# A new order for the input LayerNorm's first blocks, and two out projection tiles in two parts each

## What is computed

```python
x = layer_norm(x, ln_in_g, ln_in_b)                 # the input LayerNorm
proj = x @ w_in                                     # 1024 -> 2304 columns, four token mixers read them
...
out = jnp.concatenate([ya, yb, yc, yd], axis=-1) @ w_out     # yc is the attention's quarter
x = layer_norm(ALPHA * x + mix, ln1_g[l], ln1_b[l])
x = layer_norm(ALPHA * x + sq_relu_mlp(x, w_ff1[l], w_ff2[l]), ln2_g[l], ln2_b[l])
```

## Time and profile before

| what | value |
|---|---|
| median of 3 runs | 2541.54 us (2541.16 to 2541.88) |
| the profiled execution, its own time | 2545.45 us |
| span of its trace | 2542.7 us |
| TensorE busy | 2468.5 us, 97% of the span |
| VectorE, ScalarE busy | 1532.5 us (60%), 1285.3 us (51%) |
| share of TensorE in the chain that ended last | 91% |
| DMA | 339.08 MB, mean 133 GB/s |

### The profile page before, as it was taken

One profiled execution on the slowest core, in us unless ns is written; L12 is line 12 of the kernel. 1 busy time (PEld: TensorE's weight loads), 2 busy tenths in 40 slices (PEclk: granted clock), 3 DMA queues, 4 the chain that ended last, 5 costly groups with the idle time before them and its releaser, 6 DMA issues.

```text
span 2542.7 us, 37277 instructions
## 1 busy us (share of the span) xinstructions
PE 2468.5 (97%) x13647; PEld 2381.2 (94%) x13647; DVE 1532.5 (60%) x2210; ACT 1285.3 (51%) x1985; POOL 201.1 (8%) x403
## 2 busy tenths in 40 slices
PE   4999999979999999999999999999999999999996
PEld 4999999979999999999999999999999999999996
DVE  6535661645677767777766776755755654564435
ACT  4556522535656645566554565653445555344432
POOL 0012230000000000100100000000022130000001
PEclk9999999989999999999999999999999999999998
DMA  7434453433444333443443443433466574343332
GB/s 214 161 103 140 156 186 103 125 103 98 143 118 133 113 114 117 124 136 108 133 120 94 141 135 105 129 111 108 151 199 192 194 225 144 107 134 116 110 117 76
DMA packets 136066, 339.08 MB, mean 133 GB/s; under 512 B 20029, under 2 KB 63550, under 8 KB 135758
## 3 DMA queue, kind: packets, MB, share of 16 engines
q1 hardware_dynamic: 123534, 300.29, 38.8%
q0 software_dynamic: 12352, 36.42, 4.6%
HBM read 291.72 MB, written 44.92 MB: 132 GB/s over the span
## 4 chain that ended last, share of the span: by engine, by line
PE 91%; DVE 3%; ACT 2%; DMA 1%; issue 1%; SPq 0%; DVEq 0%; ACTq 0%
PE PS L977 21%; PE PS L978 21%; PE PS L979 20%; PE PS L745 5%; PE PS L746 5%; PE PS L747 5%; PE PS L798 2%; PE PS L820 1%; PE PS L819 1%; PE PS L882 1%; PE PS L786 1%; PE PS L785 1%; PE PS L912 1%; PE PS L870 1%; PE PS L988 1%
## 5 line engine op out<-in xcount | busy, mean ns | idle before, releaser
L1261 ACT ACTIVATE w_hi<-w_raw 128x1024 fp32r<-128x1024 f32 x239 | 251.6, 1053 | 297.3 <-PE PS L979 294.8
L977 PE MATMUL PS<-a_hi,w_hi 128*128 128x416 f32 x1072 | 385.0, 359 | 2.6 <-DVE a_lo L1905 1.4
L978 PE MATMUL PS<-a_lo,w_hi 128*128 128x416 f32 x1072 | 378.4, 353 | 0.0
L979 PE MATMUL PS<-a_hi,w_lo 128*128 128x416 f32 x1072 | 377.5, 352 | 0.0
L1784 DVE TENSOR_TENSOR w_lo<-w_raw,w_hi 128x1024 fp32r<-128x1024 f32 x239 | 291.4, 1219 | 78.0 <-ACT w_hi L1261 77.7
L977 PE MATMUL PS<-h_hi,w_hi 128*128 128x416 f32 x848 | 304.6, 359 | 0.1
L978 PE MATMUL PS<-h_lo,w_hi 128*128 128x416 f32 x848 | 298.4, 352 | 0.0
L979 PE MATMUL PS<-h_hi,w_lo 128*128 128x416 f32 x848 | 297.8, 351 | 0.0
L1809 DVE TENSOR_TENSOR h_lo<-h_full,h_hi 128x416 fp32r<-128x416 f32 x160 | 94.6, 591 | 237.4 <-ACT h_hi L1274 237.2
L977 PEld LDWEIGHTS PS<-a_hi,w_hi 128*128 128x128 f32 x1072 | 204.6, 191 | 6.7 <-issue 4.0
L979 PEld LDWEIGHTS PS<-a_hi,w_lo 128*128 128x128 f32 x1072 | 202.8, 189 | 2.2
(11 more groups left out here) (278 smaller groups left out, 5152.0 us busy)
## 6 DMA issues: line engine op xcount, KB each, us to landing
w_raw<-w_all SPq DMA_DIRECT2D x378, 512.0 KB, 3.7
proj_scratch<-stage SPq DMA_DIRECT2D x70, 208.0 KB, 2.0
k_rows<-kv_out SPq DMA_DIRECT2D x80, 128.0 KB, 4.2
x_scratch<-x_full SPq DMA_DIRECT2D x20, 416.0 KB, 2.8
x_residual<-x_scratch SPq DMA_DIRECT2D x5, 1664.0 KB, 8.8
pages<-ck SPq DMA_DIRECT2D x64, 128.0 KB, 2.1
pages<-ck POOLq DMA_DIRECT2D x64, 128.0 KB, 2.5
pages<-cv SPq DMA_DIRECT2D x64, 128.0 KB, 2.3
```

Source lines behind the costliest of these rows:

```text
L977: pe.matmul(out, w_h, mh_[:, k, :], start=(g == 0), stop=False)
L978: pe.matmul(out, w_h, ml_[:, k, :], start=False, stop=False)
L979: ins = pe.matmul(out, w_l, mh_[:, k, :], start=False, stop=(g == KT - 1))
L1261: act.activation(w_hi(n), raw[:, n % 2, :], ACT.Copy).then_inc(s_wh, 1)
```

## The change

There are two parts.

**The begin.** (1) `ident_r`, the copy that waited for the constants, stands later on DVE, and ACT's first root reads the zeroed `gsel` in place of `ident`, so neither engine waits for the constants ahead of block 0's statistics; both wait for them ahead of `block_back(0)`. (2) A second buffer `x_full_2` takes the feature tiles 4 to 7 of all blocks but the last; there are four store semaphores in place of two, and the waits for a place are in `place_free`. (3) The transposes of block 1 stand ahead of step 3 (tiles 0 to 3) and in the middle of step 3 (tiles 4 to 7); for the later blocks they stand before the third and the fourth weight tile of the block ahead. (4) In block 0's stage ACT and DVE split the weight tiles 1, 2 and 3 ahead of block 1's normalisation, and ACT empties the banks of steps 0 and 1 between them. In later blocks ACT empties two banks before `block_std` in place of one. SP's order of stores follows.

**The out projection.** (5) Steps 0 and 1 are done in two parts each: six feature tiles of step 0, six of step 1, then the attention's two of step 0 and of step 1. (6) ACT and DVE split the weights of step 2 ahead of `split_y(0, 3)`, the attention's quarter.

```diff
@@ SyncE: stores and loads of the begin
                 if b:
                     store_stage(b * GRP - 1)
                 store_stage(b * GRP)
+                if b == 0:
+                    load_raw(5)
+                store_stage(b * GRP + 1)
+                if b == 0:
+                    store_stage(b * GRP + 2)
                 store_x1(b + 1, 0)
                 store_x1(b + 1, 2)
-                store_stage(b * GRP + 1)
-                if b == 0:
-                    load_raw(5)
+                if b:
+                    store_stage(b * GRP + 2)
+                if b + 3 < NB:
+                    load_rows(b + 3)
                 store_x1(b + 1, 4)
                 store_x1(b + 1, 6)
-                if b + 3 < NB:
-                    load_rows(b + 3)
-                store_stage(b * GRP + 2)
@@ the places of x_full
+        def x_full(b, k, n=1):
+
+            t = xf2 if b < NB - 1 and k >= 4 else xf
+            return t[:, k % 4:k % 4 + n, :] if n > 1 else t[:, k % 4, :]
...
+        def place_free(eng, other, b, k):
+
+            i = k // 2
+            if b == NB - 1 and k < 2:
+                for n in (2, 3):
+                    eng.wait_ge(s_t1st[n], 16 * (NB - 1))
+            if b == NB - 1 and i >= 2:
+                eng.wait_ge(s_t1st[i - 2], 16 * NB)
+                eng.wait_ge(other, b * KT + k - 3)
+            elif b:
+                eng.wait_ge(s_t1st[i], 16 * b)
+                eng.wait_ge(other, (b - 1) * KT + k + 1)
@@ TensorE: transposes and projection steps
-                    if b + 1 < NB and p in (1, 2):
-                        for k in range(4 * p - 4, 4 * p):
+                    if 0 < b < NB - 1 and p >= 2:
+                        for k in range(4 * p - 8, 4 * p - 4):
                             turn_back(b + 1, k)
-                    project(b * GRP + p)
+                    if b == 0 and p == 3:
+                        for k in range(4):
+                            turn_back(1, k)
+                    project(b * GRP + p, turned=range(4, KT) if b == 0 and p == 3 else ())
@@ TensorE: out projection
-                dense(n)
+                if n == 0:
+                    for groups in (range(6), range(6, KT)):
+                        dense(0, groups)
+                        dense(1, groups)
+                elif n > 1:
+                    dense(n)
@@ ScalarE: the begin
-            act.wait_ge(s_const, 32)
-            act.activation(std[0:ROW, :], ident[0:ROW, 0:NR], ACT.Sqrt).then_inc(s_root, 1)
+            act.wait_ge(s_mzero, 1)
+            act.activation(std[0:ROW, :], gsel[0:ROW, 0, 0, 0:NR], ACT.Sqrt).then_inc(s_root, 1)
             wait_apart(act, s_root, 1)
             block_std(0)
             block_norm(0)
             split_hi(0)
+            act.wait_ge(s_const, 32)
             block_back(0, range(KT))
             split_hi(1)
-            for b in range(NB - 1):
+            put_out(0)
+            split_hi(2)
+            put_out(1)
+            split_hi(3)
+            block_std(1)
+            block_norm(1)
+            put_out(2)
+            block_back(1, range(KT))
+            for b in range(1, NB - 1):
                 j = b * GRP
-                if b:
-                    put_out(j - 1)
+                put_out(j - 1)
+                put_out(j)
                 block_std(b + 1)
                 block_norm(b + 1)
-                if b == 0:
-                    split_hi(2)
-                put_out(j)
+                put_out(j + 1)
                 block_back(b + 1, range(4))
-                if b == 0:
-                    split_hi(3)
-                put_out(j + 1)
+                put_out(j + 2)
                 block_back(b + 1, range(4, KT))
-                put_out(j + 2)
@@ ScalarE, VectorE: weights of step 2 (VectorE the same with lo_ahead)
+            hi_ahead(2)
             split_y(0, 3)
...
-                hi_ahead(n + 2)
+                if n:
+                    hi_ahead(n + 2)
@@ VectorE: the begin
-            dve.wait_ge(s_const, 32)
-            dve.tensor_copy(ident_r[:, :], ident[:, :]).then_inc(s_sel, 1)
             block_var(0)
             block_nmr(0)
             split_lo(0)
+            dve.wait_ge(s_const, 32)
             block_back(0, range(KT))
             split_lo(1)
+            split_lo(2)
             block_var(1)
+            block_nmr(1)
+            split_lo(3)
+            dve.tensor_copy(ident_r[:, :], ident[:, :]).then_inc(s_sel, 1)
             for b in range(NB - 1):
-                block_nmr(b + 1)
-                if b == 0:
-                    split_lo(2)
-                block_back(b + 1, range(4))
-                if b == 0:
-                    split_lo(3)
-                block_back(b + 1, range(4, KT))
+                if b:
+                    block_nmr(b + 1)
+                block_back(b + 1, range(KT))
                 if b + 2 < NB:
                     block_var(b + 2)
```

More of the change, by code:

```diff
@@ L372, in build @@
         s_wh, s_wl = sem("w_hi_made"), sem("w_lo_made")
-        s_xin, s_t1st = [sem("xin_in_a"), sem("xin_in_b")], [sem("x1_stored_a"), sem("x1_stored_b")]
+        s_xin, s_t1st = [sem("xin_in_a"), sem("xin_in_b")], [sem(f"x1_stored{n}") for n in range(4)]
         s_ve, s_std, s_nmr = sem("var_made"), sem("std_made"), sem("nmr_made")
@@ L499, in store_x1 @@
                 sp.wait_ge(s_xfd, b * 4 + k // 2 + 1)
-                sp.dma_start(x1_d[k:k + 2, :, b * BLK:(b + 1) * BLK].rearrange("k p t -> p k t"), xf[:, k % 4:k % 4 + 2, :]).then_inc(s_t1st[k // 2 % 2], 16)
+                sp.dma_start(x1_d[k:k + 2, :, b * BLK:(b + 1) * BLK].rearrange("k p t -> p k t"), x_full(b, k, 2)).then_inc(s_t1st[k // 2], 16)
             def store_stage(j):
@@ L729, in turn_back, with project @@
                 ins.then_inc(s_bt, 1)
-            def project(j, amid=()):
+            def project(j, amid=(), turned=()):
                 p, b = P_STEPS[j]
@@ L743, in project @@
                             attention(tau)
+                        for d in turned:
+                            turn_back(1, d)
                     w_h, w_l = wp_hi(p)[:, k * P:(k + 1) * P], wp_lo(p)[:, k * P:(k + 1) * P]
@@ L955, in free_bank, with dense @@
                     pe.wait_ge(s_oev, b * KT + i + 1)
-            def dense(n):
+            def dense(n, groups=range(KT)):
                 kind, b, q, i = step_at(n)
-                pe.wait_ge(s_wl, n + (NC_IN + 1))
-                if n >= 3:
-                    free_bank(n - 3)
+                if 0 in groups:
+                    pe.wait_ge(s_wl, n + (NC_IN + 1))
+                    if n >= 3:
+                        free_bank(n - 3)
                 order = KORD if kind == "out" or (kind == "up" and q == 3 and i == KT - 1) else range(KT)
@@ L965, in dense @@
                 out = PS[:, n % 3, 0:BLK]
-                for g, k in enumerate(order):
+                for g in groups:
+                    k = order[g]
                     if b == 3 and n >= base_of(3) and g == 4:
@@ L981, in dense @@
                         ins.then_inc(s_afree, 1)
-                ins.then_inc(s_step, 1)
+                if KT - 1 in groups:
+                    ins.then_inc(s_step, 1)
             def forward(src, e, j, lnb):
@@ L1120, in block_back @@
                     if k % 2 == 0:
-                        q = b * 4 + k // 2
                         act.wait_ge(s_bt, b * KT + k + 1)
-                        if q >= 2:
-                            act.wait_ge(s_t1st[q % 2], 16 * (q // 2))
-                            act.wait_ge(s_xl, b * KT + k - 3)
-                        act.activation(xf[:, k % 4, :], PS[:, 4 + k % 4, 0:BLK], ACT.Identity, bias=ln_gb[:, 1, k:k + 1],
+                        place_free(act, s_xl, b, k)
+                        act.activation(x_full(b, k), PS[:, 4 + k % 4, 0:BLK], ACT.Identity, bias=ln_gb[:, 1, k:k + 1],
                                        scale=ln_gb[:, 0, k:k + 1]).then_inc(s_xfa, 1)
@@ L1130, in block_back @@
                         act.wait_ge(s_xfd, b * 4 + k // 2 + 1)
-                    act.activation(x_hi(b)[:, k, :], xf[:, k % 4, :], ACT.Copy).then_inc(s_xh, 1)
+                    act.activation(x_hi(b)[:, k, :], x_full(b, k), ACT.Copy).then_inc(s_xh, 1)
             def put_out(j):
@@ L1520, in block_back @@
                     if k % 2:
-                        q = b * 4 + k // 2
                         dve.wait_ge(s_bt, b * KT + k + 1)
-                        if q >= 2:
-                            dve.wait_ge(s_t1st[q % 2], 16 * (q // 2))
-                            dve.wait_ge(s_xh, b * KT + k - 3)
-                        dve.tensor_scalar(xf[:, k % 4, :], PS[:, 4 + k % 4, 0:BLK], ln_gb[:, 0, k:k + 1], ln_gb[:, 1, k:k + 1],
+                        place_free(dve, s_xh, b, k)
+                        dve.tensor_scalar(x_full(b, k), PS[:, 4 + k % 4, 0:BLK], ln_gb[:, 0, k:k + 1], ln_gb[:, 1, k:k + 1],
                                           ALU.mult, ALU.add).then_inc(s_xfd, 1)
@@ L1529, in block_back @@
```

(5 more changed lines are left out.)

8 lines of the change are left out of this document (5 added, 3 removed).

## The result

| what | value |
|---|---|
| before, beside it | 2541.71 us median of 4 (2541.16 to 2544.41) |
| changed | 2522.24 us median of 4 (2521.36 to 2522.45) |
| ratio | 0.9924, 95% interval 0.9912 to 0.9936 |
| the changed kernel's profiled execution | own time 2522.45 us, span 2520.6 us |

The medians are 19.5 us apart, the ratio says 19 (16 to 22); 21.3 were forecast, and the time lies 2.0 us above the forecast one, inside the range. TensorE is now busy for 2463.3 us, 98% of the span.

The account below looks back on a forecast made before the run. TensorE, busy 97% of the span, was taken as the bound, so only its idle or half-clock time could be gained. 5.2 + 10.0 + 6.1 = 21.3 us off 2545.45, less 3.91 to the median, gave 2520.2; range 2517 to 2528.

Parts of the forecast that it names:

- The front term (5.2): Begin: block 0's statistics start as rows land, first transpose at 15.8 in place of 21.03; gain 5.2 us (4.2 to 6.3).
- The early bound: Begin: rows' last byte in at about 9.4, from 1.70 MB of rows and 1.85 MB moved by 10.00 us.
- The late bound: Begin: rows landed by 11.5, when `ident`, issued behind them, landed in the trace before.
- The rest of the begin (10.0): First transpose to block 2's transposes: these begin at 39.6, not 45.0, with six steps done, not five; gain 10.0 us.
- Later blocks, one step later: Blocks after block 2: next rows at T + 13.7, wanted at T + 15.0; slack 1.3 us, nothing lost.
- The out projection (6.1): Out projection to step 2: 3.4 us of work moved into the wait and 2.7 of clock kept; gain 6.1 us.
- 2.7 is nearer the first: Out projection: clock stays at 2.4 GHz through a 2.7 us wait, as through 1.42, unlike 5.85.
- rival (a): Out projection: the clock falls in the shortened wait; 18.6 us gained, 2522.9 us; 3 in 10.
- (b): Begin: clock rises late, step 0 wholly at 1.2 GHz, some 3.3 us lost; 2523.5, with (a) 2526.2; 1 in 10.
- (e): No effect: the begin's gain meets something fixed later, such as the attention's transfers; 2541.5 us; 3 in 100.
- (c): Begin: rows of block 2 or weight tile 3 land late, three more us on two waits; gain 15.3, 2526.2; 1 in 10.
- the late landing: Begin: block 0's rows land at the late bound, 11.5, not 10.5; front gain 4.2 in place of 5.2.

Follow-up runs that it names:

- rows_alone: Changed kernel with every load behind the constants held back until block 0's last row tile has landed; one run, 2525.05 us.
- const_wait2: Changed kernel with both engines again waiting for the constants ahead of block 0's statistics (part 1 undone); 2527.35 us, ratio 0.9944.
- front_only: Kernel before with part 1 alone (no wait for the constants ahead of block 0's statistics); 2537.85 us, ratio 0.998.
- one_x_full: Changed kernel with a single x_full of four places (part 2 undone); 2528.87 us, ratio 0.9947.
- out_only: Kernel before with the out projection parts 5 and 6 alone; 2538.64 us, ratio 0.9987.
- three_tiles: Changed kernel with the first three out projection tiles in two parts each in place of two; 2522.41 us, ratio 0.9919.

## Why the prediction was right, and where it was off

**The front term (5.2) was mis-sized: 3.5.** Its step was "I take the middle, 10.5", for the landing of the last row tile, between 9.4 and 11.5. It landed at 12.11, outside both bounds; over the ten executions with the new front it was 11.39 to 12.11, and the first transposes of the new front and of the old (20.62 to 21.46) lie 3.1 to 4.7 apart, under 5.2 in every pairing. The early bound had two errors: it took every byte moved by 10 us as a byte of the rows, and the last byte as the landing. The windows of the changed kernel (columns as in the earlier trace rows) and its DMA issues have:

```profile
0.00:10.00 10.00, 0.00 (x0) 0.00 (x0) 3.40 (x7) 1.49 (x2) 0.70 (x6) 1.00 0.72 174
```

```profile
ident<-ident_d SPq DMA_DIRECT2D x1, 64.0 KB, 9.5
```

By 10 us 1.74 MB had moved here, but that counts all transfers, so it does not say when the 1.70 MB of rows were through. In `rows_alone` they were not through at 10.0, with 1.67 MB moved in all, and the receipt followed 0.5 to 1.5 us behind the last byte. The late bound was `ident`, issued behind the rows and landed at 11.5 before; now it was issued at 2.65 and landed 9.5 later, at 12.15, in the same moment as the last row tile. Here the small transfer behind the large ones was no bound with room in it: it landed when they did (within 0.5 us in each of the ten executions). The middle of the two bounds, 10.5, was the choice that failed; 11.5, the late bound itself, is inside what the executions show.

The other two parts of the term held: 1.29 against 1.2 for the last statistics, and 17.49 - 12.11 - 1.29 = 4.09 against 4.1 behind them. `const_wait2`, 3.1, and `front_only`, 4.2, bracket the measured 3.5. The Trainium skill (DMA: Bandwidth & Descriptors, on where the fixed cost goes) has most of some 2 us pass between last byte and semaphore; `rows_alone` shows 0.5 to 1.5.

**The rest of the begin (10.0) came out at 10.2**, and its steps came out as worked out. Counted from the first transpose, measured and (forecast): block 1's statistics at 13.0 (13.2), wait ahead of step 1 0.74 (1.0), block 1's transposes at 21.9 (22.0) behind 1.49 (1.6), block 2's at 39.3 (39.6) behind 0.71 (1.1), `x_lo` of block 1 complete at 46.77 + 1.24 - 17.49 = 30.5 (30.8). That the second buffer only pays for tile 2's place was right for block 0. What the prediction did not see is that block 1's turn in the middle of a step would wait for stored places again without it (`one_x_full`, 3.43 us); that left its sum as it was, since nothing of the change was left out.

**Later blocks, one step later: nothing lost**, as forecast. There is no wait for `rows_a` or `rows_b` beyond block 2's.

**The out projection (6.1) came out at 4.7.** Its step "2.7 is nearer the first" (that a wait of 2.7 us keeps the clock as one of 1.42 does) failed: the clock fell in the shortened wait, rival (a). 3.4 us of work moved into the wait, as worked out (the wait went from 5.85 to 2.24, where 2.7 was forecast). The half clock cost 1.6 (the 12 matmuls from 500.68 to 504.56 took 3.88 us, at full pace 12 x 0.189 = 2.27) where it had cost 2.7, so 1.1 came back and not 2.7. Over the traces with this wait its length alone did not decide it: the clock fell behind 2.22, 2.24, 2.45, 2.50, 2.52 and 2.55 us, and held behind 2.17 (`const_wait2`) and 2.38 (`one_x_full`). Two waits in the begin say the same: it fell behind 1.95 (`out_only`, at 30.89) and held behind 2.24 (`one_x_full`, at 27.47).
The Trainium skill (TensorE: Matmul & The Clock Gate, on oscillation) has only longer idle gaps throttle the array, and was read as speaking for a kept clock. The traces do not agree: waits of 2.2 to 2.6 us between full-pace matmuls were mostly enough, and so was 1.89 in `three_tiles`.

**The sum**: 3.5 + 10.2 + 1.0 + 4.7 = 19.5 against 5.2 + 10.0 + 0 + 6.1 = 21.3. The two misses, 1.7 and 1.4, have one sign, and the 1.0 us that only the execution before lost balances part of them. Rival (a), 2522.9, is the case that happened; (b) to (e) did not: step 0 ran at full pace, no load was late (ACT made weight tile 3's high part at 33.81 without a wait), and no later stage began to wait. Two of the marks that the prediction set for the new profile were missed by a little, both by the terms above: the first transpose at 17.49 (15 to 17), and the wait of 2.24 (2.5 to 3).

**From the trace to the median.** The prediction took 3.91 us off, as the execution before lay that far above its median, and so took for granted that the new execution would too. It lay 0.2 above. Part of the 3.91 was the wait of 0.74, and part may be the 2.8 us at half pace behind the LayerNorm, which differ between executions of one kernel. By the executions' own times the gain was 23.0, more than forecast, and by the medians 19.5, less; that 2520.2 is so near is partly luck.

**The upper end of the range does not follow from its sum.** (b) 3.3, (c) 6.0, (a) 2.7 and the late landing 1.0 make 13.0 us, which is 2533 and not 2528. Only without (c) does it come to 2527. The measured time is inside either way.

What stays open is why the clock falls behind one wait and not behind a longer one in another kernel.

## What to carry to other kernels

Ahead of a long wait, first look for work of the waiting engine that needs only something small from the others (here two weight tiles) and put both earlier; price the buffer that this order needs in every block that it changes, not only where the old wait stood. Put the landing of a transfer at its last byte plus the receipt, and count for its last byte only its own bytes. Do not reckon a shortened wait's clock as given back: in the begin and the out projection of these kernels it held through every wait up to 1.67 us and fell behind eight of the eleven between 1.89 and 2.55. Fill the wait if there is one more independent tile. And before a trace's gain is set beside the medians, ask how far each profiled execution lies from its own median.

## What the runs showed of the hardware

- Four row tiles of 416 KB in one queue landed 1.95 to 2.43 us apart (2.08 in `rows_alone`), the last one in `rows_alone` 0.5 to 1.5 us after its last byte.
- A 64 KB transfer issued behind them landed together with the last of them (12.15 against 12.11; within 0.5 us in all ten executions).
- The granted clock fell to 0.50 behind eight of eleven waits of TensorE of 1.89 to 2.55 us, and the fall came between about the wait's end and 1.5 us after it. It held behind 2.17, 2.24 and 2.38.
- Two executions of one program had the same waits to 0.31 us and yet half-clock stretches of different lengths at the same place (behind the LayerNorm, 6.8 and 17.1 us), worth some 3 us.
